# The first two weight units of a two-block transformer kernel fed by a host-turned x in eight pieces

## The chip, the cores and the metric

The kernel runs on one core of one Trainium2 chip. The metric is the device time of one execution in microseconds (us); of several runs the median is shown. The engines are TensorE (PE in the profile, PEld its weight loads), VectorE (DVE), ScalarE (ACT), GpSimd (POOL) and SyncE (SP), whose queue issues most of the loads from HBM.

## The reference, cut

One transformer block with two kinds of attention, and behind it two layers of a second kind. The change touches only the beginning of the first block: its norm over rows of x, and the product with `w_in`.

```python
def rms_norm(x, g):
    xf = x.astype(jnp.float32)
    y = xf * lax.rsqrt(jnp.mean(xf * xf, axis=-1, keepdims=True) + NORM_EPS)
    return (y * g.astype(jnp.float32)).astype(x.dtype)

u = rms_norm(h, norm_mix_g[l])                  # h = x, 256 x 1024
z = u @ w_in[l]                                 # 1024 x 5640
qa, ka, va, qk_b, vb, ob, ib, fb, ga, gb = jnp.split(z, IN_SPLITS, axis=-1)
...
i_pre = (ib + b_igate[l].astype(ib.dtype)).transpose(0, 2, 1)
f_pre = (fb + b_fgate[l].astype(fb.dtype)).transpose(0, 2, 1)
```

`ib` and `fb` are the eight gate columns of `z`. They go through a log-sigmoid and a running sum into the second attention's weights.

## The kernel before

All weights are read once, in units of 1 MB (128 partitions x 2048 float32 numbers), 227 in all. They pass through three slots: SP loads a unit into `raw`, ScalarE rounds it into `whi` (float32r), VectorE takes the rest `raw - whi` into `wlo`. TensorE forms each product from three matmuls, x_hi w_hi, x_lo w_hi and x_hi w_lo. A slot is loaded again when its `wlo` has been made (`lo_done`, in the function `fill`). A unit is 24 matmuls of 512 columns on TensorE.

Units 0 and 1 are the two halves (by rows) of `w_in`'s first 512 columns (q of the first attention), units 2 and 3 those of the next 512 (k), units 4 and 5 those of v, units 6 to 9 four narrow units of 256 columns. In the code they are called QA, KA, VA and QKB. The row factor of the norm, `rstd`, is not applied to x but later, to the products, when ScalarE copies them out of PSUM. Only the gain (`gcol`) is multiplied into x, together with its turning: TensorE transposes x (`turn_x`, four row-by-column blocks to a PSUM bank), ScalarE writes `xhi` out of PSUM and VectorE `xlo` (both in `turned_gain`).

x arrives as rows, in two halves by columns; between them come the first quarters of unit 0. TensorE first runs matmuls on zeros (`idle`), then turns the first half of x, then runs six more zero matmuls, then unit 0 in two halves (`wide_halves`), with the second half of x turned between them. Then come the eight gate matmuls (L2056: the columns of `wif` against all of x), then unit 1, then one small transpose of the convolution's weights (L2061) and two small matmuls (L2065) that add up and place the gate values. The latter wait for the table of constants (`cst_full`), which ScalarE's queue loads, 532 KB.

Each engine runs its own instructions in the order in which the code writes them; there is no scheduler. So these orders are fixed behind the head. VectorE: gate inputs (L1357, L1361), the low part of unit 4 (L1021), small steps, the rotation of q (four times L1113, L1115, L1117), the low part of unit 5, then the gates' second part that ends with four products with the identity (L1330, into `turned_a`), then the low part of unit 6. ScalarE: high part of unit 4 (L648), exp and ln of the gates (L831, L833, with a table load), the copies of q out of PSUM (L820), high part of unit 5. TensorE uses `turned_a` in L2084, which stands between units 4 and 5. GpSimd computes `rstd` from the sums of squares, makes a diagonal matrix of it (L561) and then issues some twenty small loads.

Of the kernel before, what the change touches and what calls it, by code (L numbers as in the profile page):

```python
# [11 lines left out]
ACT = mybir.ActivationFunctionType  # L12
# [3 lines left out]
P = 128  # L16
# [47 lines left out]
TURN_BANKS = {T_MIX: (4, 5, 6, 7), T_Y0: (4, 5, 2, 3), T_M0: (0, 1, 5, 7), T_M1: (0, 1, 5, 7)}  # L64
# [86 lines left out]
def turns_of(T):  # L151

    return 4 * T - (2 if T > T_Y0 else 0)
# [33 lines left out]
def build(nc, t, out):  # L187
# [7 lines left out]
    with ExitStack() as ctx:  # L195
# [113 lines left out]

        rbc0, gate_t = memT[:, 0, :], memT[0:16, 2, :]  # L310
# [39 lines left out]
        quarter_hi, quarter_full = sem("quarter_hi"), sem("quarter_full")  # L350
        half_full = [sem(f"half_full{u}") for u in range(2)]
        half_hi, half_lo = sem("half_hi"), sem("half_lo")
        x_full = [sem(f"x_full{h}") for h in range(2)]
# [46 lines left out]
        def _(sp):  # L400
# [44 lines left out]
            def half_unit(u, h, s):  # L445
                k = 4 * u + 2 * h
                sp.dma_start(raw[:, u, 1024 * h:1024 * h + 1024].rearrange("p (a b) -> p a b", a=2),
                             cols(w_in, k, 2, 0, 512)).then_inc(s, 16)

            for h in range(2):  # L450
                for r in range(RT):
                    v = slice(512 * h, 512 * h + 512)
                    sp.dma_start(res[:, r, v], t["x"][0, r * P:(r + 1) * P, v]).then_inc(x_full[h], 16)
                if h == 0:
                    for k, s in enumerate((quarter_full, half_full[0])):
                        sp.dma_start(raw[:, 0, 512 * k:512 * k + 512], w_in[P * k:P * k + P, 0:512]).then_inc(s, 16)
                    half_unit(0, 1, raw_full[0])
# [6 lines left out]
            wide(KA, w_in, 512)  # L464
# [29 lines left out]
        def _(pool):  # L494
# [64 lines left out]
            pool.wait_ge(rstd_ready, 2)  # L559
            for r in range(RT):  # L560
                pool.tensor_scalar(rdg0[:, r, :], ident, rstd[:, r:r + 1], None, ALU.mult).then_inc(diag0_ready, 1)  # L561
# [78 lines left out]
        def _(act):  # L640
# [147 lines left out]

            act.dma_start(cst[:, 0:P], t["consts"][:, 0:P]).then_inc(ident_full, 16)
            act.dma_start(gcol[:, :], t["gcol"]).then_inc(gcol_full, 16)  # L790

            act.wait_ge(pool_chain, 2)
            act.activation(cf[:, 3:4], mhalf[:, :], ACT.Square)
            def hi_half(u, h):
                v = slice(1024 * h, 1024 * h + 1024)
                if u == 0 and h == 0:

                    v = slice(512, 1024)
                act.wait_ge(raw_full[u] if h else half_full[u], 16)
                act.activation(whi[:, u, v], raw[:, u, v], ACT.Copy).then_inc(hi_done if h else half_hi, 1)  # L800
# [11 lines left out]
            turned_gain(T_MIX, N_MIX, 1)  # L812
            hi_half(1, 0)
            hi_half(1, 1)
            act.dma_start(cst[:, P:C_W], t["consts"][:, P:C_W]).then_inc(cst_full, 16)
            hi(2, 2)
# [5 lines left out]
            for u in range(PROJ):  # L822
# [3 lines left out]
                if u < PROJ - 1:  # L826
                    hi(u + 3, u % 3)
# [180 lines left out]
        def _(dve):  # L1008
# [260 lines left out]

            def lo_half(u, h):  # L1270
                v = slice(1024 * h, 1024 * h + 1024)
                dve.wait_ge(hi_done if h else half_hi, u + 1)
                dve.tensor_tensor(wlo[:, u, v], raw[:, u, v], whi[:, u, v], ALU.subtract)\
                    .then_inc(lo_done if h else half_lo, 1)

            dve.wait_ge(gcol_full, 16)
            dve.wait_ge(quarter_full, 16)
            dve.tensor_copy(whi[:, 0, 0:512], raw[:, 0, 0:512]).then_inc(quarter_hi, 1)
            turned_gain(T_MIX, N_MIX, 0, (0, 1))
# [1048 lines left out]
```

## Time and profile before

| what | value |
|---|---|
| median of 3 runs | 1345.19 us (1344.61 to 1345.22) |
| profiled execution, its own time | 1344.8 us |
| its span | 1343.0 us |
| TensorE busy | 1337.7 us, 100% of the span |
| VectorE busy | 1072.4 us, 80% |
| ScalarE busy | 702.1 us, 52% |
| HBM read | 244.45 MB, 183 GB/s over the span |

The span runs from the first instruction to the last; the own time holds 1.8 us more, which lie around it. Busy shares are means over the whole span. In this kernel they say little on the head, which is the first 60 us.

### The profile page before, as it was taken

Reading aid. Unit: us, or ns where it says so; the run is one execution under the profiler, and the core shown is the slowest. Engines: PE = TensorE matmul, PEld = TensorE weight load, DVE = VectorE, ACT = ScalarE, POOL = GpSimd, SP = SyncE. Lnnn points to the kernel's source line nnn. Section 1 sums busy time; section 2 is a strip of 40 time slices with the busy share of each in tenths; the row PEclk is TensorE's granted clock in tenths of the full one; section 3 lists DMA queues with packets and bytes.
Section 4 is the critical chain, followed back from the end, with each engine's and each line's share of the span. In section 5 each row is a group of like instructions: output and inputs, shape, how many; then the busy total and the mean of one; then the engine's idle time right before and its main releaser. Section 6 shows DMA issues by size and latency. Waiting matters only on the chain.

```text
span 1343.0 us, 17790 instructions
## 1 busy us (share of the span) xinstructions
PE 1337.7 (100%) x6477; PEld 1107.4 (82%) x6477; DVE 1072.4 (80%) x1882; ACT 702.1 (52%) x937; POOL 123.6 (9%) x158
## 2 busy tenths in 40 slices
PE   9999999999999999999999999999999999999999
PEld 7988888888888888887888888888888888888887
DVE  6994678877878877968778888898888788698777
ACT  5566446444454444577664444544445677644442
POOL 4042000020010000042000000000000332100000
PEclk9999999999999999999999999999999999999999
DMA  9654455675555555554346555465556542455562
GB/s 275 214 160 149 165 172 189 232 262 198 199 173 195 199 199 190 178 179 142 124 145 230 193 187 188 157 220 188 187 188 209 167 158 94 147 200 192 199 202 93
DMA packets 108818, 246.41 MB, mean 183 GB/s; under 512 B 5113, under 2 KB 9637, under 8 KB 108625
## 3 DMA queue, kind: packets, MB, share of 16 engines
q1 hardware_dynamic: 106576, 240.19, 53.0%
q0 software_dynamic: 1744, 4.70, 1.3%
q8 instruction: 40, 0.66, 0.2%
q10 hardware_dynamic: 432, 0.66, 0.1%
q14 instruction: 26, 0.21, 0.0%
HBM read 244.45 MB, written 1.07 MB: 183 GB/s over the span
## 4 chain that ended last, share of the span: by engine, by line
PE 97%; DVE 1%; ACT 0%; issue 0%; DMA 0%; POOL 0%; SPq 0%; DVEq 0%
PE ps L1728 27%; PE ps L1676 17%; PE ps L1678 17%; PE ps L1677 17%; PE ps L1733 14%; PE ps L1921 1%; PE ps L1702 1%; PE ps L1975 1%; PE ps L1959 1%; PE ps L2244 0%; DVE wlo L1533 0%; DMA res<-in_x 0%; PE ps L2010 0%; PE ps L2016 0%; PE ps L2020 0%
## 5 line engine op out<-in xcount | busy, mean ns | idle before, releaser
L1728 PE MATMUL ps<-whi,xx 128*128 128x512 f32 x1600 | 379.2, 389 | 0.0
L1728 PEld LDWEIGHTS ps<-whi,xx 128*128 128x128 f32 x1600 | 300.3, 188 | 62.2
L648 ACT ACTIVATE whi<-raw 128x2048 fp32r<-128x2048 f32 (+1 forms) x165 | 261.9, 1599 | 85.9 <-PE ps L1678 50.0
L1021 DVE TENSOR_TENSOR wlo<-raw,whi 128x2048 fp32r<-128x2048 f32 x105 | 240.0, 2289 | 50.6 <-ACT whi L648 49.8
L1224 DVE STREAM_TRANSPOSE sc<-sc 32x128 f32<-32x128 f32 x864 | 261.7, 303 | 12.9
L1026 DVE TENSOR_TENSOR wlo<-raw,whi 128x2048 fp32r<-128x2048 f32 x90 | 206.1, 2290 | 46.8 <-ACT whi L656 45.5
L656 ACT ACTIVATE whi<-raw 128x2048 fp32r<-128x2048 f32 x90 | 171.8, 1909 | 64.5 <-PE ps L1733 64.5
L1676 PE MATMUL ps<-whi,hhi 128*128 128x512 f32 (+1 forms) x506 | 198.3, 392 | 0.0
L1733 PE MATMUL ps<-wlo,xx 128*128 128x512 f32 x800 | 197.6, 389 | 0.0
L1678 PE MATMUL ps<-whi,hlo 128*128 128x512 f32 (+1 forms) x506 | 196.7, 389 | 0.0
L1677 PE MATMUL ps<-wlo,hhi 128*128 128x512 f32 (+1 forms) x506 | 196.5, 388 | 0.0
L1676 PE MATMUL ps<-whi,xx 128*128 128x512 f32 x464 | 187.6, 404 | 0.3 <-DVE xx L1551 0.3
L1678 PE MATMUL ps<-whi,xx 128*128 128x512 f32 x464 | 181.5, 391 | 0.0
L1677 PE MATMUL ps<-wlo,xx 128*128 128x512 f32 x464 | 180.8, 390 | 0.0
L1733 PEld LDWEIGHTS ps<-wlo,xx 128*128 128x128 f32 x800 | 150.2, 188 | 31.2
L747 ACT ACTIVATE hhi<-sc 128x512 fp32r<-128x512 f32 x54 | 34.2, 634 | 212.6 <-DVE sc L1224 212.6
L1678 PEld LDWEIGHTS ps<-whi,hlo 128*128 128x128 f32 x506 | 95.0, 188 | 19.8
L1676 PEld LDWEIGHTS ps<-whi,hhi 128*128 128x128 f32 x506 | 95.1, 188 | 19.3 <-DVE hlo L1229 0.4
L1677 PEld LDWEIGHTS ps<-wlo,hhi 128*128 128x128 f32 x506 | 95.1, 188 | 19.1
L1678 PEld LDWEIGHTS ps<-whi,xx 128*128 128x128 f32 x464 | 87.1, 188 | 19.1
L1676 PEld LDWEIGHTS ps<-whi,xx 128*128 128x128 f32 x464 | 87.3, 188 | 17.4 <-issue 1.1
L1677 PEld LDWEIGHTS ps<-wlo,xx 128*128 128x128 f32 x464 | 87.4, 188 | 16.1
(285 smaller groups left out, 1150.0 us busy)
## 6 DMA issues: line engine op xcount, KB each, us to landing
raw<-in_ffn_gate_up SPq DMA_DIRECT2D x88, 1024.0 KB, 5.2
raw<-in_ffn_w_down SPq DMA_DIRECT2D x44, 1024.0 KB, 5.0
raw<-in_w_in SPq DMA_DIRECT2D x40, 1024.0 KB, 5.1
raw<-in_gate_up SPq DMA_DIRECT2D x22, 1024.0 KB, 5.3
raw<-in_w_out SPq DMA_DIRECT2D x12, 1024.0 KB, 4.9
raw<-in_w_down SPq DMA_DIRECT2D x11, 1024.0 KB, 5.0
raw<-in_w_mem_kv SPq DMA_DIRECT2D x4, 1024.0 KB, 5.3
raw<-in_w_proj_a SPq DMA_DIRECT2D x2, 1024.0 KB, 5.2
```

What stands on the lines that cost most here:

```text
L648: ins = act.activation(whi[:, slot, v], raw[:, slot, v], ACT.Copy)
L656: act.activation(whi[:, c % 3, :], raw[:, c % 3, :], ACT.Copy).then_inc(hi_done, 1)
L747: act.activation(hhi[:, par, :], hidT, ACT.Copy).then_inc(h_hi, 1)
L1021: dve.tensor_tensor(wlo[:, u % 3, v], raw[:, u % 3, v], whi[:, u % 3, v], ALU.subtract)\
L1026: dve.tensor_tensor(wlo[:, c % 3, :], raw[:, c % 3, :], whi[:, c % 3, :], ALU.subtract)\
L1224: ins = dve.transpose(dst[32 * a:32 * a + 32, :, b, :], src[32 * b:32 * b + 32, :, a, :])
L1676: pe.matmul(o, stat[0], mov[0], start=start, stop=False)
L1677: pe.matmul(o, stat[0], mov[1], start=False, stop=False)
L1678: return pe.matmul(o, stat[1], mov[0], start=False, stop=stop)
L1702: ins = pe.transpose(ps[:, bank, a:a + P], res[:, r, P * c:P * c + P], ident)
L1728: pe.matmul(ps[:, banks[r], :], x(4 * half + k, P * r, P)[part], whi[:, slot, 512 * k:512 * k + 512], start=half == 0 and k == 0 and part ...
L1733: ins = pe.matmul(ps[:, banks[r], :], x(4 * half + k, P * r, P)[0], wlo[:, slot, 512 * k:512 * k + 512], start=False, stop=half == 1 and k ...
```

## The change

- The host gives x a second time, turned: `x_t`, 128 x 8 x 256. It is loaded in eight pieces of 128 KB into the tile `memT` (called `xt` there), and each is followed in SP's queue by a piece of 256 KB of unit 0 or 1.
- ScalarE makes `xhi` of a piece from `xt` by a copy with the gain as scale, and VectorE `xlo`; TensorE's 16 transposes, and the last six zero matmuls with one of the first eight, are gone.
- TensorE multiplies piece by piece: high, low weights of the piece before, low x.
- x in rows, which the sums of squares and the residual still need, is loaded behind unit 2. Unit 2 and unit 3 are now loaded and split in halves, and unit 3 stands behind x.
- The gate matmuls come behind unit 1 and not behind unit 0; the two small matmuls (L2065) come behind unit 2 and not ahead of it. VectorE's gate inputs stand ahead of unit 4's low part as before.
- In ScalarE's queue `gcol` is issued ahead of the identity. The constants are issued behind the wait for x in rows.

```diff
+            for c in range(KC):
+                x_part(c)
+                w_part(c // 4, c % 4)
             sp.dma_start(wif[:, :, :], t["wif"]).then_inc(wif_full, 16)
-            half_unit(1, 0, half_full[1])
-            half_unit(1, 1, raw_full[1])
+            half_unit(KA, 0)
+            half_unit(KA, 1)
+            for r in range(RT):
+                sp.dma_start(res[:, r, :], t["x"][0, r * P:(r + 1) * P, :]).then_inc(x_full, 16)
...
+            half_unit(KA + 1, 0)
+            half_unit(KA + 1, 1)
             wide(VA, w_in, 1024)
...
             act.wait_ge(gcol_full, 16)
-            turned_gain(T_MIX, N_MIX, 0, (0, 1))
-            hi_half(0, 0)
-            turned_gain(T_MIX, N_MIX, 0, (2, 3))
-            hi_half(0, 1)
+            for c in range(KC):
+                act.wait_ge(xt_full[c], 16)
+                act.activation(xhi[:, c, :], xt[:, c, :], ACT.Copy, scale=gain_col(N_MIX, c)).then_inc(xhi_done, 1)
+                if c < KC - 1:
+                    hi_part((c + 1) // 4, (c + 1) % 4)
             act.wait_ge(wif_full, 16)
             act.activation(wifs[:, :, 0:8], wif[:, :, :], ACT.Copy).then_inc(wif_hi, 1)
-            act.wait_ge(x_full[0], 16 * RT)
-            act.wait_ge(x_full[1], 16 * RT)
+            hi_half(KA, 0)
+            hi_half(KA, 1)
+            act.wait_ge(x_full, 16 * RT)
...
+            for c in range(KC):
+                dve.wait_ge(xhi_done, c + 1)
+                dve.scalar_tensor_tensor(out=xlo[:, c, :], in0=xt[:, c, :],
+                                         scalar=gain_col(N_MIX, c), in1=xhi[:, c, :], op0=ALU.mult, op1=ALU.subtract)\
+                    .then_inc(xlo_done, 1)
+                lo_part(c // 4, c % 4)
...
+                if u == 0:
+                    gate_sums()
+                    lo_half(KA + 1, 0)
+                    lo_half(KA + 1, 1)
+                if u == 1:
+                    gate_inputs()
+                if 0 < u < 7 and u != 4:
                     lo(u + 3)
...
-            idle(8)
...
+            idle(7)
...
-            pe.wait_ge(ident_full, 16)
-            turn_x(0)
-            idle(6)
+            for c in range(KC):
+                high(c)
+                if c > 0:
+                    w_low(c - 1)
+                x_low(c)
+            w_low(KC - 1)
```

TensorE's first instructions, before the change (`pr` is the tile of zeros, `res` is x in rows, `xx` holds `xhi` and `xlo`):

```order
L1983 MATMUL ps<-pr 128x128 [waits warm_ready]
L1983 MATMUL ps<-pr 128x128 x7
L1994 MATMUL ps<-cst,res 128x128 [waits x_full0,ident_full]
L1994 MATMUL ps<-cst,res 128x128 x7
L1983 MATMUL ps<-pr 128x128 x6
L2010 MATMUL ps<-whi,xx 128x512 [waits xhi_done,quarter_hi]
```

And of the change:

```order
L2019 MATMUL ps<-pr 128x128 [waits warm_ready]
L2019 MATMUL ps<-pr 128x128 x6
L2035 MATMUL ps<-whi,xx 128x512 [waits xhi_done,quarter_hi]
L2035 MATMUL ps<-whi,xx 128x512
L2041 MATMUL ps<-whi,xx 128x512 [waits xlo_done]
L2041 MATMUL ps<-whi,xx 128x512
L2035 MATMUL ps<-whi,xx 128x512 [waits xhi_done,part_hi]
```

The transposes and the second run of zeros are gone; after the second pair TensorE waits for a second piece.

TensorE around the end of unit 1, before the change (L1676 is the first matmul of unit 2):

```order
L2020 MATMUL ps<-wlo,xx 128x512 x3
L2061 MATMUL ps<-cst,cwr 128x32 [waits bias_full]
L2065 MATMUL ps<-cst,memT 128x8 [waits gate_copied,cst_full]
L2065 MATMUL ps<-cst,memT 128x8
L1676 MATMUL ps<-whi,xx 128x512 [waits lo_done]
```

Of the change, from the end of unit 2 to unit 3's first matmul:

```order
L1714 MATMUL ps<-whi,xx 128x512
L2105 MATMUL ps<-cst,memT 128x8 [waits gate_copied,cst_full]
L2105 MATMUL ps<-cst,memT 128x8
L2111 MATMUL ps<-memT,cst 128x128 [waits diag0_ready]
L2111 MATMUL ps<-memT,cst 128x128
L1712 MATMUL ps<-whi,xx 128x512 [waits half_lo]
```

The two small gate matmuls (L2065, now L2105) stand one whole unit later.

VectorE around the gates, before the change (`small` holds the gates):

```order
L1294 COPY memT<-ps 16x256 [waits gate_ps]
L1296 TENSOR_TENSOR memT<-memT,ps 16x256 [waits gate_copied]
L1021 TENSOR_TENSOR wlo<-raw,whi 128x2048 [waits hi_done] x2
L1357 SCALAR_TENSOR_TENSOR small<-ps,rstd,bif 128x8 [waits gate_ps,bias_full,rstd_ready]
L1357 SCALAR_TENSOR_TENSOR small<-ps,rstd,bif 128x8
```

Of the change, from the sums of squares to unit 4's low part:

```order
L1318 ISA xn,ss<-res 128x1024 [waits x_full]
L1318 ISA ss 128x1
L1323 COPY memT<-ps 16x256 [waits gate_ps]
L1325 TENSOR_TENSOR memT<-memT,ps 16x256 [waits gate_copied]
L1301 TENSOR_TENSOR wlo<-raw,whi 128x1024 [waits half_hi]
L1301 TENSOR_TENSOR wlo<-raw,whi 128x1024 [waits hi_done]
L1332 SCALAR_TENSOR_TENSOR small<-ps,rstd,bif 128x8 [waits gate_ps,bias_full,rstd_ready]
L1332 SCALAR_TENSOR_TENSOR small<-ps,rstd,bif 128x8
L1336 SCALAR_TENSOR_TENSOR small<-small 128x8 [waits gate_dve]
L1338 TENSOR_SCALAR small<-small 128x8
L1038 TENSOR_TENSOR wlo<-raw,whi 128x2048 [waits hi_done,dve_chain]
```

The gate inputs keep their place ahead of unit 4's low part, but what they wait for on TensorE has moved; the gates' sums now stand ahead of unit 3's low part.

## Rows read from the trace of the kernel before

**Rows 1.** The page: the span, TensorE's busy time, and its clock by slices.

```profile
span 1343.0 us, 17790 instructions
...
PE 1337.7 (100%) x6477; PEld 1107.4 (82%) x6477; DVE 1072.4 (80%) x1882; ACT 702.1 (52%) x937; POOL 123.6 (9%) x158
...
PEclk9999999999999999999999999999999999999999
```

**Rows 2.** TensorE's waits, the second longest: us in total, times, longest.

```profile
PE ps L1921 <- DVE sc L1188: 0.5, 1, 0.5
```

**Rows 3.** Timeline, first 11 us: start, us, engine, line, operation, tiles.

```profile
1.06 3.79 PE L1983 MATMUL ps<-pr 128*128 128x128 f32 x16 [1.06 <-DVE pr L1268]
...
5.08 1.41 PE L1994 MATMUL ps<-cst,res 128*128 128x128 f32 x8 [0.24 <-DMA res<-in_x]
...
5.67 0.43 DVE L1278 CAST whi<-raw 128x512 fp32r<-128x512 f32 x1 [4.67 <-DMA raw<-in_w_in]
...
6.33 1.50 PE L1983 MATMUL ps<-pr 128*128 128x128 f32 x12
...
6.90 0.62 ACT L800 ACTIVATE whi<-raw 128x512 fp32r<-128x512 f32 x1
...
7.59 1.17 PE L2010 MATMUL ps<-whi,xx 128*128 128x512 f32 x4
...
10.44 1.03 PE L1994 MATMUL ps<-cst,res 128*128 128x128 f32 x8
```

**Rows 4.** Timeline, 14 to 28 us, TensorE.

```profile
14.05 2.01 PE L2056 MATMUL ps<-xx,wifs 128*16 128x512 f32 x8
...
21.53 0.59 PE L2065 MATMUL ps<-cst,memT 16*128 16x8 f32 x4
...
22.04 0.50 PE L1676 MATMUL ps<-whi,xx 128*128 128x512 f32 x1
...
27.62 0.60 PE L2071 MATMUL ps<-memT,cst 128*128 128x128 f32 x4
```

**Rows 5.** Timeline, 24 to 29 us, VectorE and ScalarE.

```profile
24.14 1.92 ACT L648 ACTIVATE whi<-raw 128x2048 fp32r<-128x2048 f32 x1 [2.21 <-DMA raw<-in_w_in]
...
24.18 0.35 DVE L1357 SCALAR_TENSOR_TENSOR small<-ps,rstd,bif 128x8 f32<-128x8 f32 x2
...
24.57 0.17 DVE L1361 SCALAR_TENSOR_TENSOR small<-small 128x8 f32<-128x8 f32 x1
...
25.97 0.19 ACT L831 ACTIVATE small<-small 128x8 f32<-128x8 f32 x1
...
28.87 0.69 DVE L1113 TENSOR_TENSOR sq<-work,cst 128x512 f32<-128x512 f32 x1 [0.23 <-ACT work L820]
```

**Rows 6.** Timeline, 36 to 40 us.

```profile
36.12 2.50 DVE L1330 TENSOR_TENSOR turned_a<-cst,small 128x512 fp32r<-128x512 f32 x4
...
39.23 2.29 DVE L1021 TENSOR_TENSOR wlo<-raw,whi 128x2048 fp32r<-128x2048 f32 x1 [0.61 <-ACT whi L648]
...
39.46 1.10 PE L2084 MATMUL ps<-turned_a,hhi 128*128 128x512 f32 x4
```

**Rows 7.** Timeline, 49 to 54 us.

```profile
49.87 2.29 DVE L1021 TENSOR_TENSOR wlo<-raw,whi 128x2048 fp32r<-128x2048 f32 x1
...
53.29 0.36 PE L1676 MATMUL ps<-xx,whi 128*128 128x256 f32 x1
```

**Rows 8.** DMA issues of two short windows: count, KB each, median us to landing.

```profile
raw<-in_w_in SPq DMA_DIRECT2D x1, 256.0 KB, 3.9
...
cst<-in_consts ACTq DMA_DIRECT2D x1, 532.0 KB, 6.6
```

**Rows 9.** Stretches: engines' busy time, granted clock, DMA share, GB/s.

```profile
0.00:5.00 5.00, 3.79 (x16) 3.49 (x16) 0.17 (x1) 1.49 (x2) 0.32 (x6) 1.00 0.64 188
...
8.00:16.00 8.00, 8.00 (x41) 5.91 (x40) 7.38 (x13) 6.29 (x12) 3.63 (x6) 1.00 1.05 383
...
26.00:34.00 8.00, 8.00 (x41) 6.75 (x40) 7.47 (x10) 4.88 (x8) 0.58 (x2) 1.00 1.01 162
```

More of the change, by code:

```diff
@@ L151, in turns_of @@
 def turns_of(T):
-    return 4 * T - (2 if T > T_Y0 else 0)
+    return 4 * T - (6 if T > T_Y0 else 4)
 def s_bank(i):
@@ L794, in hi_half @@
             def hi_half(u, h):
+                act.wait_ge(raw_full[u % 3] if h else half_full[u - KA], 16 * (u // 3 + 1) if h else 16)
+                if u == 3 and h == 0:
+                    act.wait_ge(unit_used, 1)
                 v = slice(1024 * h, 1024 * h + 1024)
[L796 to L800, printed above, removed]
+                act.activation(whi[:, u % 3, v], raw[:, u % 3, v], ACT.Copy).then_inc(hi_done if h else half_hi, 1)
@@ L825, in _ @@
                     evac_pT(8)
-                if u < PROJ - 1:
+                if u == 0:
+                    hi_half(KA + 1, 0)
+                    hi_half(KA + 1, 1)
+                elif u < PROJ - 1:
                     hi(u + 3, u % 3)
@@ L1268, in _, with lo_part @@
             dve.memset(pr[:, 0, 0:P], 0.0).then_inc(warm_ready, 1)
+            def lo_part(u, k):
+                if u == 0 and k == 0:
+                    dve.wait_ge(quarter_hi, 1)
+                elif k == 3:
+                    dve.wait_ge(hi_done, u + 1)
+                else:
+                    dve.wait_ge(part_hi, k + 1 + 2 if u else k)
+                v = slice(512 * k, 512 * k + 512)
+                dve.tensor_tensor(wlo[:, u, v], raw[:, u, v], whi[:, u, v], ALU.subtract)\
+                    .then_inc(lo_done if k == 3 else part_lo, 1)
@@ new lines, in gate_inputs @@
+            def gate_inputs():
+                dve.wait_ge(rstd_ready, 2)
+                dve.wait_ge(bias_full, 48)
+                dve.wait_ge(gate_ps, 3)
+                for r in range(RT):
+                    ins = dve.scalar_tensor_tensor(out=gates[:, r, :], in0=ps[:, 4, 8 * r:8 * r + 8],
+                                                   scalar=rstd[:, r:r + 1], in1=bif[:, :], op0=ALU.mult, op1=ALU.add)
+                ins.then_inc(gate_dve, 1)
+                dve.wait_ge(gate_dve, 1)
+                dve.scalar_tensor_tensor(out=rh(0), in0=f_pre, scalar=-1.0, in1=f_pre, op0=ALU.mult, op1=ALU.max)\
+                    .then_inc(gate_dve, 1)
+                link(dve.tensor_scalar(rh(72), f_pre, 0.0, None, ALU.min))
@@ L1985, in _ @@
             pe.wait_ge(warm_ready, 1)
-            idle(8)
-            def turn_x(half):
-                pe.wait_ge(x_full[half], 16 * RT)
-                for b in (2 * half, 2 * half + 1):
-                    for c in (2 * half + b, 2 * half + b + 2):
-                        bank, a = turn_at(T_MIX, c)
-                        for r in range(RT):
-                            ins = pe.transpose(ps[:, bank, a + P * r:a + P * r + P], res[:, r, P * c:P * c + P], ident)
-                    ins.then_inc(tr_ps, 1)
@@ L2026, in _, with high @@
-            pe.wait_ge(ident_full, 16)
-            turn_x(0)
-            idle(6)
+            idle(7)
+            def high(c):
+                u, k = c // 4, c % 4
+                if c == 0:
+                    pe.wait_ge(quarter_hi, 1)
+                elif k == 3:
+                    pe.wait_ge(hi_done, u + 1)
+                else:
+                    pe.wait_ge(part_hi, k + 3 if u else k)
+                pe.wait_ge(xhi_done, c + 1)
+                for r in range(RT):
+                    pe.matmul(ps[:, r, :], x(c, P * r, P)[0], w(u, 512 * k, 512)[0], start=c == 0, stop=False)
@@ new lines, in x_low, with w_low @@
+            def x_low(c):
+                pe.wait_ge(xlo_done, c + 1)
+                for r in range(RT):
+                    pe.matmul(ps[:, r, :], x(c, P * r, P)[1], w(c // 4, 512 * (c % 4), 512)[0], start=False, stop=False)
+            def w_low(c):
+                u, k = c // 4, c % 4
+                pe.wait_ge(lo_done if k == 3 else part_lo, u + 1 if k == 3 else 3 * u + k + 1)
+                for r in range(RT):
+                    ins = pe.matmul(ps[:, r, :], x(c, P * r, P)[0], w(u, 512 * k, 512)[1], start=False, stop=c == KC - 1)
+                if k == 3:
+                    ins.then_inc(unit_used, 1)
@@ L2308 @@
     given["wif"] = np.asarray(inputs["w_in"])[0][:, 3584:3592].reshape(KC, P, 2 * BH).transpose(1, 0, 2)
+    given["x_t"] = np.asarray(inputs["x"])[0].reshape(SEQ, KC, P).transpose(2, 1, 0)
     given["mem_t"] = np.asarray(inputs["mem_2"])[0].reshape(SEQ, KC, P).transpose(2, 1, 0)
```

132 lines of the change are left out of this document (49 added, 83 removed).

## The prediction

> **What bounds the kernel now.** The page first [rows 1]: TensorE is busy for 1337.7 of 1343.0 us, with the clock granted in full in every slice. Then its waits [rows 2]: behind the start the longest is 0.5 us in all. So anything TensorE does earlier, and keeps, comes off the end; nothing else does. What can be kept is decided in the head, so I went to the timeline.
>
> TensorE runs zero matmuls from 1.06 us, turns x from 5.08, runs zeros again from 6.33 and starts unit 0 at 7.59 [rows 3]. From there it never stops: the second turning at 10.44 [rows 3], gates at 14.05, unit 2 at 22.04, and that unit's 24 matmuls end at 27.62, so 5.58 us a unit and 0.2325 us a matmul [rows 4]. What could be gained is what stands ahead of 22.04 and is not a weight matmul.
>
> Then I looked for the place where another engine is nearly late. It is between units 4 and 5. TensorE's product with `turned_a` starts at 39.46. VectorE has finished writing that tile at 36.12 + 2.50 = 38.62 [rows 6]. That is 0.84 us of slack. The next is unit 7, whose low part ends at 49.87 + 2.29 = 52.16 for a matmul at 53.29 [rows 7], 1.13 us. VectorE is occupied nearly without a break between 28.9 and 52, so this work comes earlier only if its first link does. That link is the rotation at 28.87, which waits for q's copy by ScalarE. The copy stands behind ln and exp of the gates, exp at 25.97, which stands behind the high part of unit 4 (24.14 to 26.06) and behind the gate inputs (24.18, the last that matters ends at 24.57 + 0.17 = 24.74) [rows 5]. Those need TensorE's two small gate matmuls, done at 21.53 + 0.59 = 22.12 [rows 4].
>
> **The change, part by part.**
>
> *Start.* The first `w` piece is now SP's second load, with 0.13 MB ahead of it; before it was the third, issued at 1.65 us, with 0.52 MB ahead, and was there for the cast at 5.67 [rows 3, 8]. It is issued 0.45 us earlier, and about 0.4 MB less lies ahead, which at 0.35 MB per us is 1.1 us. If only the issue counts it lands at 5.2, if both count in full at 4.1; I take the smaller amount of data alone, 4.5, since in these first us the bytes are what fills the time. The cast costs 0.43 [rows 3]: first matmul at 5.0 instead of 7.59 (4.6 to 5.7). The x piece and `gcol`, now first in its queue, are there by then.
>
> *The first two pieces.* The sixteen rows of zeros from 1.06 took 3.79 us, the twelve from 6.33 took 1.50 [rows 3]: 0.237 against 0.125 each, the levels of 1.2 and 2.4 GHz. The rise came between 5.1 and 6.3, after 4 us of nearly unbroken work. So the first four matmuls run at about 0.46 us and end at 6.8. The second weight piece lands about 1.1 us behind the first, at 5.6; ScalarE then needs 0.62 for it [rows 3] and about 0.43 for its x: 6.7. TensorE goes on at 6.8, and at the upper level from here.
>
> *Steady pieces.* A piece is 0.393 MB, 1.06 us at 0.37 MB per us (a little under the 383 GB/s of 8 to 16 us [rows 9], as a third of it comes in rows of 1 KB). ScalarE and VectorE need about 1.05 us each. TensorE needs 6 x 0.2325 = 1.40 us. It sets the pace: 44 matmuls are 10.2 us, to 17.0. Eight gate matmuls, 1.86, and the small transpose, 0.1: unit 2 starts at 19.0 and not at 22.04. Unit 2 ends at 24.6, the small gate matmuls, now here, at 25.1, and unit 3 starts at about 25.4. The 16 transposes and the zeros are thus worth 2.6 us at this place.
>
> *Loads.* 0.94 MB are in by 5 us (188 GB/s x 5 [rows 9]); the eight pieces and `gcol`, 3.25 MB, by 11.2; unit 2 by 13.9; x in rows by 16.7; unit 3 by 19.4. One more MB is loaded than before, but units 2 and 3 come ahead of their use by 5 us, which covers their split in halves (about 1 us on ScalarE and 1.2 us on VectorE a half). The constants are issued when x is in, at 16.7. They took 6.6 us before [rows 8], issued then as now into a queue with two units in front: 23.3, and with unit 4 (1.6 MB, 4.2 us) all is in by 23.6. They are wanted at 24.6. I cost this at nothing. If they come later, every us counts, as all of the gates' chain stands behind it. GpSimd's diagonal and its twenty small loads move back by about 5 us; nobody waits for them before unit 3.
>
> *The chain.* The gate inputs now start when TensorE is done with the small matmuls, at 25.1, and not at 24.18. Exp can follow 0.6 us later, at 25.7, instead of 25.97. The other condition, unit 4's high part, ends at 23.6 + 1.9 = 25.5. So the rotation starts about 0.27 us earlier, not 2.6, and `turned_a` is ready at about 38.35. TensorE would want it at 39.46 - 2.6 = 36.9. It waits some 1.5 us there. The gain that passes is 0.84 + 0.27 less about 0.1 for the handover: **1.0 us**. At unit 7 VectorE has lost its 0.61 us of idle [rows 6], so its work is 0.9 us ahead and the slack of 1.13 holds. From there on VectorE follows TensorE, and the gain stays to the end.
>
> The sum: 1344.8 of the profiled execution less 1.0 is 1343.8. The median of the runs was 1345.19, 0.4 above it, so I say **1344.2**.
>
> *A rule against pieces.* The rows show loads of 256 KB landing 3.9 us after their issue [rows 8] while others are issued meanwhile. The Trainium skill, "DMA: Bandwidth & Descriptors", Anatomy of one DMA, gives each DMA about 2 us that do not depend on its size, and puts the half-efficient size at some 860 KB; these pieces are far below. By that rule alone, sixteen loads one behind the other would take about 39 us (an estimate from the page), and the head would lose some 25 us instead of gaining. The stretch of 383 GB/s is against it.
>
> **The rivals.**
>
> *The whole head gain passes.* If the slack at `turned_a` or the order on VectorE is not what I read, the end moves by 2.6: 1342.6. For it: TensorE waits for nothing now. Against: the 0.84 us are plain arithmetic on two rows. Chance 0.10.
>
> *The clock rises late.* TensorE now has a gap from about 4.3 to 5.0 and perhaps one at 6.5, where it had 0.24 us idle before [rows 3]. Each us that the rise comes after 6.8 costs half a us, with nothing to hide it, since the chain hangs on TensorE. If it comes as late as 11.5, the loss is 2.35: 1.0 - 2.35, so 1346.6, slower than before. It decides from 2 us behind 6.8 on. The Trainium skill, "TensorE: Matmul & The Clock Gate", What's actually happening, says that the gate follows how busy the array has lately been; by that rule the gaps matter, and the rise may shift from run to run. In the trace a gap did not stop it. Chance 0.13.
>
> *The constants are late.* If GpSimd's small loads, which ran beside a stretch of only 162 GB/s at 26 to 34 us [rows 9], slow this stretch instead, the 1.6 MB of unit 4 and constants from 19.4 need 9.9 us: 29.3 and not 23.6. The small matmuls come 4.7 us late, and the result is 3.7 slower: 1348.9. It is slower than before as soon as they land after 25.6. A mild form, 0.5 to 1.5 us late, gives 1344.7 to 1345.7. Chance 0.11, a third of it the full form.
>
> *The pieces come one by one.* Each load waits for the one before: sixteen times 3.9 us, 62 us instead of 11: some 50 us slower, 1395. Chance 0.01.
>
> **How the numbers follow.** My forecast has 0.63; its own range is 1343.6 (first piece at 4.1 and unit 4 loaded 0.4 earlier) to 1344.9 (first piece at 5.2). The remaining 0.02 is unnamed. The range reaches down to the full gain and up to the late clock: 1342.4 to 1346.6, which leaves out less than 2 in 10. Two tenths of a per cent, 2.7 us, is about what a measurement of this kernel tells from no change. Faster by that needs under 1342.5, the lower half of the first rival and a little: 0.06. Slower needs over 1347.9: the full form of the constants, a still later clock, the serial pieces, 0.07. Within: 0.87.
>
> **What would show it.** Right: the first 512-column matmul at 5.0; a pause of up to 0.3 us behind the fourth; unit 2 at 19.0, unit 3 at 25.4; the small gate matmuls not waiting for a load; the list of waits with a new line, TensorE for VectorE's `turned_a`, of about 1.5 us; that product at 38.4. Wrong: no such wait and `turned_a` written before 37; a wait on the constants; zeros' successors at 0.46 us beyond 8 us; or TensorE waiting for pieces 2 to 7. The time would be wrong without a change in mechanism if the waits of later blocks, small now, should grow.

## The result, and the profile after

The changed kernel takes 1346.76 us (median of 20 runs, 1345.66 to 1348.41), the kernel before 1344.64 (20 runs, 1344.22 to 1345.95). The ratio is 1.0016, with a 95% interval of 1.001 to 1.0022: 2.1 us slower, and 0.16 us above the range. The prediction had added 0.4 us to its sum because the three runs that it had of the kernel before had their median at 1345.19; over 20 runs that median is 1344.64, so against its own base the range ended 1.4 us above the kernel before, and the changed kernel is 2.1 above it. The profiled execution took 1347.21 us, 2.4 more than the 1344.8 of the one before.

The page of the changed kernel, the lines that answer to [rows 1]:

```profile
span 1345.4 us, 17755 instructions
...
PE 1337.4 (99%) x6447; PEld 1105.7 (82%) x6447; DVE 1072.7 (80%) x1888; ACT 703.6 (52%) x942; POOL 124.2 (9%) x158
...
PEclk9999999999999999999999999999999999999999
```

TensorE's busy time is down by only 0.3 us, though 16 transposes and 14 rows of zeros are gone. (It counts matmuls at the lower clock with their full length.) Its waits (us in total, times, longest) show what is new:

```profile
PE ps L2124 <- DVE turned_a L1372: 1.4, 1, 1.4
PE ps L2035 <- DVE whi L1306: 1.1, 1, 1.1
...
PE ps L2035 <- ACT xx L821: 0.4, 1, 0.4
```

The first is the wait that was forecast. The other two are in the first 8 us. The changed kernel's timeline there, and to 20 us (start, us, engine, line, operation):

```profile
1.06 3.36 PE L2019 MATMUL ps<-pr 128*128 128x128 f32 x14 [1.06 <-DVE pr L1285]
...
5.05 0.43 DVE L1306 CAST whi<-raw 128x512 fp32r<-128x512 f32 x1 [4.05 <-DMA raw<-in_w_in]
...
5.53 1.22 PE L2035 MATMUL ps<-whi,xx 128*128 128x512 f32 x2 [1.12 <-DVE whi L1306]
...
6.55 1.05 PE L2041 MATMUL ps<-whi,xx 128*128 128x512 f32 x2
6.87 0.63 ACT L809 ACTIVATE whi<-raw 128x512 fp32r<-128x512 f32 x1 [2.09 <-DMA raw<-in_w_in]
...
8.04 1.19 PE L2035 MATMUL ps<-whi,xx 128*128 128x512 f32 x2 [0.43 <-ACT xx L821]
...
9.03 1.05 PE L2048 MATMUL ps<-wlo,xx 128*128 128x512 f32 x2
...
9.88 1.05 PE L2041 MATMUL ps<-whi,xx 128*128 128x512 f32 x2
...
10.74 1.05 PE L2035 MATMUL ps<-whi,xx 128*128 128x512 f32 x2
...
12.26 0.63 PE L2041 MATMUL ps<-whi,xx 128*128 128x512 f32 x2
...
12.73 0.63 PE L2035 MATMUL ps<-whi,xx 128*128 128x512 f32 x2
...
20.02 2.01 PE L2095 MATMUL ps<-xx,wifs 128*16 128x512 f32 x8
```

Pairs that start 0.86 us apart (9.03, 9.88, 10.74) are at 1.2 GHz, pairs 0.47 apart (12.26, 12.73) at 2.4. So the level rose at about 12.0 us. The clock row of the page and of the windows reads full here from the start; only the spacing of the rows shows the level. From 12.26 on, 34 matmuls take 7.76 us, 0.228 each, without a wait.

The changed kernel, 19 to 43 us. The rows answer to [rows 4 to 6]:

```profile
19.12 1.06 ACT L829 ACTIVATE xn<-res 128x1024 f32<-128x1024 f32 x1 [1.50 <-DMA res<-in_x]
...
22.14 0.50 PE L1712 MATMUL ps<-whi,xx 128*128 128x512 f32 x1
...
26.99 1.91 ACT L660 ACTIVATE whi<-raw 128x2048 fp32r<-128x2048 f32 x1 [3.08 <-DMA raw<-in_w_in]
...
27.81 0.61 PE L2105 MATMUL ps<-cst,memT 16*128 16x8 f32 x4
...
28.56 0.36 DVE L1332 SCALAR_TENSOR_TENSOR small<-ps,rstd,bif 128x8 f32<-128x8 f32 x2 [3.36 <-PE ps L2105]
...
29.15 0.21 ACT L848 ACTIVATE small<-small 128x8 f32<-128x8 f32 x1 [0.24 <-DVE small L1336]
...
32.07 0.69 DVE L1130 TENSOR_TENSOR sq<-work,cst 128x512 f32<-128x512 f32 x1 [0.31 <-ACT work L834]
...
39.33 2.50 DVE L1372 TENSOR_TENSOR turned_a<-cst,small 128x512 fp32r<-128x512 f32 x4
...
41.88 1.21 PE L2124 MATMUL ps<-turned_a,hhi 128*128 128x512 f32 x4 [1.41 <-DVE turned_a L1372]
```

Unit 2 starts at 22.14; before it was 22.04 [rows 4]. All that was removed is lost again by then, and the 0.5 us of the small gate matmuls too, which no longer stand ahead of unit 2. The rotation moved from 28.87 [rows 5] to 32.07, and TensorE's product with `turned_a` from 39.46 [rows 6] to 41.88, 2.42 later. That shift stays to the end: the spans differ by 2.4.

The loads of the changed kernel (count, KB each, us to landing): the first two pieces of weights, issued at 1.17 and 2.11 us, then the constants, issued at 19.16. Behind them the stretches (engines' busy time, granted clock, DMA share, GB/s):

```profile
raw<-in_w_in SPq DMA_DIRECT2D x1, 256.0 KB, 3.8
...
raw<-in_w_in SPq DMA_DIRECT2D x1, 256.0 KB, 4.7
...
cst<-in_consts ACTq DMA_DIRECT2D x1, 532.0 KB, 7.6
```

```profile
0.00:5.00 5.00, 3.36 (x14) 3.06 (x14) 0.17 (x1) 1.99 (x3) 0.32 (x6) 1.00 0.62 164
5.00:8.00 3.00, 2.07 (x4) 1.16 (x4) 1.50 (x4) 1.09 (x3) 0.00 (x0) 1.00 1.00 354
8.00:12.00 4.00, 3.96 (x9) 3.14 (x10) 4.00 (x8) 3.96 (x8) 0.00 (x0) 1.00 1.06 379
...
20.00:24.00 4.00, 4.00 (x18) 2.36 (x17) 2.31 (x6) 2.40 (x4) 3.13 (x6) 1.00 1.06 404
24.00:28.00 4.00, 4.00 (x20) 3.06 (x18) 1.20 (x2) 1.01 (x1) 4.00 (x8) 1.00 1.02 351
```

The constants, issued at 19.2 when x had landed, took 7.6 us and were there at 26.8. Before they took 6.6 [rows 8]. The DMA engines were busy in full all that time, at 351 to 404 GB/s, so the number of bytes ahead is the likely cause of the lateness; two experiments below take bytes away.

### The profile page after: what moved, and what is told of

It reads as the page before. It is cut to its first block, busy times and chain, and to the rows that moved or that the text cites. A ratio compares the mean times of both kernels' runs of the same rounds, so it can differ in the third digit from the quotient of the medians.

```text
span 1345.4 us, 17755 instructions
## 1 busy us (share of the span) xinstructions
PE 1337.4 (99%) x6447; PEld 1105.7 (82%) x6447; DVE 1072.7 (80%) x1888; ACT 703.6 (52%) x942; POOL 124.2 (9%) x158
## 4 chain that ended last, share of the span: by engine, by line
PE 96%; DVE 2%; ACT 1%; issue 1%; DMA 0%; POOL 0%; SPq 0%; DVEq 0%
PE ps L1764 27%; PE ps L1712 17%; PE ps L1714 17%; PE ps L1713 17%; PE ps L1769 13%; PE ps L1957 1%; PE ps L1738 1%; PE ps L2011 1%; PE ps L1995 1%; PE ps L2284 0%; DVE wlo L1569 0%; DMA raw<-in_w_in 0%; PE ps L2035 0%; PE ps L2048 0%; PE ps L2041 0%
## 5 line engine op out<-in xcount | busy, mean ns | idle before, releaser
L660 ACT ACTIVATE whi<-raw 128x2048 fp32r<-128x2048 f32 (+1 forms) x163 | 258.1, 1595 | 83.0 <-PE ps L1714 50.3
L1038 DVE TENSOR_TENSOR wlo<-raw,whi 128x2048 fp32r<-128x2048 f32 x103 | 235.3, 2288 | 46.5 <-ACT whi L660 45.7
L1043 DVE TENSOR_TENSOR wlo<-raw,whi 128x2048 fp32r<-128x2048 f32 x90 | 206.0, 2289 | 46.8 <-ACT whi L668 45.7
```

The costliest lines, as they stand in the source:

```text
L660: ins = act.activation(whi[:, slot, v], raw[:, slot, v], ACT.Copy)
L1038: dve.tensor_tensor(wlo[:, u % 3, v], raw[:, u % 3, v], whi[:, u % 3, v], ALU.subtract)\
L1043: dve.tensor_tensor(wlo[:, c % 3, :], raw[:, c % 3, :], whi[:, c % 3, :], ALU.subtract)\
```

## The experiments

There are twelve kernels, in three groups (four experiments, four, four). Each was timed 11 times, and each group beside 33 runs of the kernel before, whose medians were 1344.82, 1344.87 and 1344.85 us. A time is the median, with lowest and highest, and a ratio stands to the kernel before, with its 95% interval. Two questions came first. Is it the late clock? And what does the move of the small gate matmuls cost by itself?

### Zeros in both gaps of the head

```diff
-            idle(7)
+            idle(10)
...
                 x_low(c)
+                if c == 0:
+                    for _ in range(5):
+                        pe.matmul(ps[:, 7, 0:P], pr[:, 0, 0:P], pr[:, 0, 0:P], start=True, stop=True)
```

> The changed kernel with ten pairs of zero matmuls at the start instead of seven, and five pairs on a free PSUM bank between the first and the second x piece, so that TensorE has hardly a gap before 8 us. Theory 'clock': the late rise to the upper level (12.0 us in the changed kernel) is what the head lost. Then the 512-column matmuls step at 0.23 us from about 6 us on, unit 1 ends near 18.2, unit 2 starts near 20.2, and the small gate matmuls wait for the constants (landed at 26.8): gate inputs at 26.6 to 27.5 instead of 28.56, time 1.0 to 2.0 us under the changed kernel: 1344.8 to 1345.8. Rival 'loads': the pieces come too late anyway; then the time stays within 0.5 us of the changed kernel (1346.8) whatever the clock does.

Measured: 1347.65 us (1345.56 to 1348.25), ratio 1.0014 [1.0005, 1.0023]. The head did what was expected: the first pair of unit 0 starts at 5.04 and the next at 5.61, so the level is up. But the median is not the 1344.8 to 1345.8 of the theory; it is 0.9 over the changed kernel. This kernel's timeline, 25 to 42 us:

```profile
25.80 0.61 PE L2108 MATMUL ps<-cst,memT 16*128 16x8 f32 x4
...
26.70 1.92 ACT L660 ACTIVATE whi<-raw 128x2048 fp32r<-128x2048 f32 x1 [3.14 <-DMA raw<-in_w_in]
...
28.52 0.19 ACT L848 ACTIVATE small<-small 128x8 f32<-128x8 f32 x1
...
41.22 1.88 PE L2127 MATMUL ps<-turned_a,hhi 128*128 128x512 f32 x4 [2.78 <-DVE turned_a L1372]
```

TensorE's gate matmuls are 2.0 us earlier than in the changed kernel. But exp (28.52) now stands behind the high part of unit 4, whose load is not there before 26.70. So exp is only 0.6 us earlier, and the wait for `turned_a` grows from 1.4 to 2.8 us. What follows that wait, in stretches of this kernel:

```profile
38.00:41.50 3.50, 0.72 (x3) 0.30 (x3) 3.40 (x9) 0.00 (x0) 0.00 (x0) 1.00 0.85 88
41.50:44.90 3.40, 3.40 (x9) 2.63 (x9) 3.37 (x4) 1.91 (x1) 0.00 (x0) 0.50 0.98 300
44.90:48.00 3.10, 3.10 (x15) 2.52 (x15) 3.00 (x6) 0.00 (x0) 0.00 (x0) 1.00 1.00 342
```

The granted clock is 0.50, the level of 1.2 GHz, for 3.4 us: 1.7 us lost. The times fall in two groups. Five runs with a mean granted clock of 1.000 lie at 1345.56 to 1346.19; six with 0.998 or 0.999 at 1347.65 to 1348.25. Half the clock for 3.4 us of 1346 is a mean of 0.9987, so here the mean tells one group from the other. In the five runs without a fall the median is 1345.87, 0.5 under the changed kernel's runs at a mean of 1.000 (1346.38). That is all that the filled gaps gained.

### Zeros in the first gap alone

The same, with only `idle(7)` made `idle(10)`.

> The changed kernel with ten pairs of zero matmuls at the start instead of seven; the pause behind the first piece (7.4 to 8.0 us in the changed kernel) stays. Theory 'clock, first gap': the gap of 1.1 us ahead of the first matmul alone kept the clock down: rise near 6, time as with both gaps filled, 1344.8 to 1345.8. Rival 'clock, both gaps': the pause behind the first piece, now 1.6 us long, brings it down again or keeps it down; rise near 12 again and time near 1346.8.

Measured: 1347.39 us (1345.51 to 1348.97), ratio 1.0016 [1.0007, 1.0025]. The level rose at about 4.2 us, as with both gaps filled, and stayed up through a wait of 1.6 us at 6.5. So the second gap alone doesn't bring the level down again. That the first alone caused the late rise is not shown by one profile of each (more in the part on why the prediction was wrong). The wait for `turned_a` was 1.9 us, and the clock fell again behind it, from 41.7 to 45.1. Of its runs, the five at 1.000 lie up to 1346.57 (median 1346.26, only 0.1 under the changed kernel's) and the six at 0.999 from 1347.39 on.

### The kernel before with a gap in its zeros

```diff
-            idle(8)
+            idle(5)
...
             turn_x(0)
-            idle(6)
```

> The kernel before with five pairs of zeros at the start instead of eight and none behind the first turning, so with a gap of about 1.8 us ahead of the first transpose and nothing else changed. Theory 'clock': the rise moves from 5.8 us to 9 or later, the matmuls of unit 0 step at 0.43 us, and since TensorE never waits the whole delay comes out at the end: 1.0 to 2.5 us over the kernel before (1344.6): 1345.6 to 1347.1. Rival: the level comes back by itself near 6 us and the time is that of the kernel before, or up to 0.5 less as the first matmul starts earlier.

Measured: 1345.32 us (1344.51 to 1345.94), ratio 1.0003 [0.9994, 1.0013]. The level rose at about 7.8, behind a gap of 1.2 us, and not at 9 or later, and the time is 0.5 over the kernel before and not 1.0 to 2.5: the theory missed. The five profiles that begin like the kernel before and have no such gap (its own and four of the experiments below) have the rise between 5.8 and 7.2 us, so this one is late by 0.6 to 2.

### The kernel before with the small gate matmuls behind unit 2

```diff
                     pe.transpose(ps[:, 5, 0:32], cwr[:, :], ident[0:32, 0:32]).then_inc(gate_ps, 1)
+                if u == 2:
                     pe.wait_ge(cst_full, 16)
                     pe.wait_ge(gate_copied, 2)
```

> The kernel before with one part of the change alone: the two small gate matmuls (with their wait for the constants) stand behind unit 2 and not ahead of it. Theory 'chain': the gate inputs start at 27.7 instead of 24.18, the rotation at 31.2 instead of 28.87, turned_a is ready at 40.95 instead of 38.62, TensorE waits 1.5 us for it between units 4 and 5, and the time is 1.5 us over the kernel before: 1346.1. Rival 'slack': VectorE catches up, no wait, time unchanged within 0.3 us.

Measured: 1346.76 us (1346.19 to 1347.35), ratio 1.0014 [1.0005, 1.0023]. This kernel's timeline, 27 to 42 us:

```profile
27.49 0.61 PE L2066 MATMUL ps<-cst,memT 16*128 16x8 f32 x4
...
28.23 0.36 DVE L1357 SCALAR_TENSOR_TENSOR small<-ps,rstd,bif 128x8 f32<-128x8 f32 x2 [3.81 <-PE ps L2066]
...
31.74 0.69 DVE L1113 TENSOR_TENSOR sq<-work,cst 128x512 f32<-128x512 f32 x1 [0.37 <-ACT work L820]
...
41.55 1.19 PE L2085 MATMUL ps<-turned_a,hhi 128*128 128x512 f32 x4 [1.42 <-DVE turned_a L1330]
```

With the head, the loads and the transposes of the kernel before, this one move costs 1.9 us (1.5 was expected), nearly as much as the whole change loses. TensorE here has no earlier start to set against it, and in the changed kernel's profile it had none either. The chain is the one of the prediction: gate inputs 28.23, rotation 3.51 us behind (3.51 in the changed kernel too), product 9.8 us behind that.

### Covering the wait with zeros

Eight zero matmuls ahead of the `turned_a` product: first with the zeros of the first experiment, then in the changed kernel as it is (five there). The second of the two thus has the changed kernel's head, loads and order, and shows a second execution of them.

```diff
                 if u == 4:
+                    for _ in range(8):
+                        pe.matmul(ps[:, 7, 0:P], pr[:, 0, 0:P], pr[:, 0, 0:P], start=True, stop=True)
                     pe.wait_ge(gate_dve, 5)
```

> e1_zeros_both with eight pairs of zero matmuls more, on a free PSUM bank directly ahead of the product with turned_a, so that TensorE's wait of 2.8 us there holds work. Theory 'second fall': that wait brought the clock down for 3.4 us (41.5 to 44.9 in e1's profile), worth 1.5 to 1.7 us, in about half of e1's runs (their times stand in two groups, 1345.6 to 1346.2 and 1347.7 to 1348.3). Then no fall, one group, median 1345.6 to 1346.2. Rival: the two groups come from when the loads land; then they remain and the median stays near 1347.6.

> The changed kernel with five pairs of zero matmuls directly ahead of the product with turned_a and nothing else. The profiled execution of the changed kernel had no fall of the clock there, so what remains is the late first rise: theory 'chain plus now and then a fall': the runs above 1347.5 vanish, the median moves from 1346.8 to 1346.2 to 1346.7. Rival: unchanged spread, 1345.7 to 1348.4.

Measured: 1346.24 us (1345.47 to 1347.75), 1.0012 [1.0003, 1.0021], for the first. All its 11 runs have a mean clock of 1.000, so the fall is gone. But 1346.24 is no better than the first experiment's undisturbed runs (median 1345.87), and one run of the 11 took 1347.75 without any fall. For the second: 1346.46 (1345.78 to 1348.34), 1.0014 [1.0005, 1.0023], 0.3 under the changed kernel with intervals that overlap. One run lies above 1348, so the slow runs did not vanish. Four of its 11 runs read 0.999; where the clock was low in these isn't shown. (In its profile the five zero matmuls left 0.8 us of the wait.) A late first rise is not it: the changed kernel's profile has its rise at 12.0 and reads 1.000.

The profile of the second, 1345.99, is worth more than its median. Its rows:

```profile
5.07 1.22 PE L2035 MATMUL ps<-whi,xx 128*128 128x512 f32 x2 [0.66 <-DVE whi L1306]
...
8.46 0.86 PE L2048 MATMUL ps<-wlo,xx 128*128 128x512 f32 x2
9.16 0.63 PE L2041 MATMUL ps<-whi,xx 128*128 128x512 f32 x2
...
20.38 0.50 PE L1712 MATMUL ps<-whi,xx 128*128 128x512 f32 x1
...
26.06 0.52 PEld L2105 LDWEIGHTS ps<-cst,memT 16*128 16x128 f32 x4 [0.35 <-DMA cst<-in_consts]
...
26.07 1.91 ACT L660 ACTIVATE whi<-raw 128x2048 fp32r<-128x2048 f32 x1 [3.58 <-DMA raw<-in_w_in]
...
27.89 0.19 ACT L848 ACTIVATE small<-small 128x8 f32<-128x8 f32 x1
...
30.79 0.69 DVE L1130 TENSOR_TENSOR sq<-work,cst 128x512 f32<-128x512 f32 x1 [0.23 <-ACT work L834]
```

With the same head the level rose at about 9.0 and not at 12.0, and unit 2 starts at 20.38 and not 22.14. Now the small gate matmuls do wait for the constants, and exp stands behind the high part of unit 4, whose load is not there before 26.07. The rotation is 1.28 us earlier than in the changed kernel's profile, and the time 1.22 less. It is still 1.1 over the kernel before, and that part is set by loads.

### Half a MB less ahead of unit 4

On top of the first of these two, the second half of x's rows is loaded behind unit 5. The kernel leaves out their sum of squares and takes that of the first half twice:

```diff
-            for r in range(RT):
-                sp.dma_start(res[:, r, :], t["x"][0, r * P:(r + 1) * P, :]).then_inc(x_full, 16)
+            sp.dma_start(res[:, 0, :], t["x"][0, 0:P, :]).then_inc(x_full, 16)
...
             wide(VA, w_in, 1024)
+            sp.dma_start(res[:, 1, :], t["x"][0, P:2 * P, :]).then_inc(x_late, 16)
```

> f1_zeros_wait with the second 128 rows of x loaded behind unit 5 instead of ahead of unit 3, 0.5 MB less in front of unit 4 and of the constants. The second rows' sum of squares is taken from the first rows, so the row factors of the second half are others. Theory 'loads': unit 4's load (26.6 in e1) sets exp and so turned_a; it lands 1.3 earlier, the gate inputs start near 25.5 to 26.5, exp at 27.1, and the time falls by 1.0 to 1.4 under f1: 1344.4 to 1345.0. Rival 'TensorE': the gate matmuls set it; time within 0.3 of f1.

Measured: 1345.37 us (1344.94 to 1346.28), 1.0004 [0.9995, 1.0013]. That is 0.87 less than its base, where 1.0 to 1.4 was expected; ten of its 11 runs lie under the base's median. Unit 4's high part starts at 25.70 and not 26.37, and the rotation at 30.60 and not 31.09. The bytes are a cost, a little smaller than I had said. With them gone, the gate matmuls (26.34) and unit 4 (25.70) are again about even.

### The kernel before, with its zeros removed behind the turning

`idle(8)` becomes `idle(9)` and `idle(6)` goes. Does an early start alone gain?

> The kernel before without the six pairs of zeros behind the first turning, and one pair more at the start against the gap. Unit 0 can start near 6.7 instead of 7.59. Theory 'slack at turned_a': up to 0.84 us of that pass to the end: 0.4 to 0.8 us under the kernel before. Rival 'clock': with less work ahead the level rises later and the time is the same or up to 0.5 over it.

Measured: 1344.95 us (1344.3 to 1346.38), 1.0002 [0.9993, 1.0011]: missed. This kernel's timeline, 5 to 11 us:

```profile
6.84 0.70 PE L2010 MATMUL ps<-whi,xx 128*128 128x512 f32 x2
7.98 0.70 PE L2010 MATMUL ps<-whi,xx 128*128 128x512 f32 x2 [0.44 <-ACT whi L800]
...
10.35 1.03 PE L1994 MATMUL ps<-cst,res 128*128 128x128 f32 x8
```

Unit 0 starts 0.75 us earlier than before, but waits for its second piece of weights. The second turning stands at 10.35 against 10.44 [rows 3]. The twelve rows of zeros in the kernel before had lain in time in which TensorE would have waited for the next load. Their removal brings the second turning 0.1 us forward and not the 1.5 that they take, and the median shows no gain.

### VectorE's second gate part ahead of unit 5's low part

```diff
-                if u == 3:
+                if u == 2:
                     dve.wait_ge(cst_full, 16)
                     dve.wait_ge(gate_ps, 4)
```

It was tried in three kernels: on the previous experiment, on the first one, and on the kernel before alone.

> f4_before_early with VectorE's second gate part (small steps and turned_a) ahead of unit 5's low part instead of behind it. Theory 'slack at turned_a': f4's head start of 0.75 us was swallowed there (its profile waits 0.6 us for turned_a). With the order turned, turned_a is ready 2.3 us earlier and the tightest places are unit 5 and unit 7 with 1.7 us, so the start passes: 0.5 to 0.8 us under the kernel before (1344.87): 1344.1 to 1344.4. Rival: something else holds f4, time as f4, 1344.95.

> e1_zeros_both with the same turned order on VectorE. Theory 'chain from unit 4's load': the rotation starts at 31.2 as in e1, turned_a is ready at 38.9 where TensorE wants it at 38.7, and unit 5's low part at 41.2, 0.8 later than the kernel before has unit 5 on TensorE: 0.6 to 1.1 us over the kernel before, 1345.5 to 1346.0, one group of times, no wait over 1.6 us. Rival: the second fall of the clock comes all the same; median 1347 or more.

> The kernel before with the turned order on VectorE alone. No engine waits less ahead of TensorE, which is never idle: time within 0.3 us of the kernel before. If it is slower, unit 5's low part, now 3.4 us later (38.6 for a start at 40.4), is late in some runs.

| on | us | ratio |
|---|---|---|
| before without `idle(6)` | 1344.79 (1344.57 to 1345.43) | 0.9999 [0.999, 1.0008] |
| changed, zeros in both gaps | 1345.43 (1345.02 to 1346.6) | 1.0004 [0.9995, 1.0013] |
| before | 1345.15 (1344.79 to 1345.51) | 1.0001 [0.9992, 1.001] |

In the first, `turned_a` is no longer waited for, but as said there was nothing to pass on (product at 39.20 against 39.46). In the second the median is 0.4 under the first experiment's undisturbed runs, and its 11 runs all have a mean clock of 1.000. In its profile, 1346.6 and its highest run, unit 4 came only at 27.64; the waits were 1.7 for `turned_a` and 1.0 for unit 5's low part. Here too unit 4's load sets exp (29.46). In the third the 0.3 us over the kernel before are within the noise.

### The constants split

On top of the second row of the table: two masks of the table, 0.26 MB, are loaded behind unit 5's high part (the waits for `cst_full` go to 32 with it).

```diff
-            act.dma_start(cst[:, P:C_W], t["consts"][:, P:C_W]).then_inc(cst_full, 16)
+            for a, b in ((C_TRI, C_MB), (C_INV, C_W)):
+                act.dma_start(cst[:, a:b], t["consts"][:, a:b]).then_inc(cst_full, 16)
...
+                if u == 2:
+                    for a, b in ((C_MA, C_TRI), (C_MB, C_INV)):
+                        act.dma_start(cst[:, a:b], t["consts"][:, a:b]).then_inc(cst_rest, 16)
```

> g2_zeros_swap with the two masks of the table of constants (0.26 of 0.53 MB) loaded behind unit 5's high part. Theory 'loads': 0.26 MB less ahead of unit 4 and the constants, unit 4 lands 0.7 earlier, exp and the rotation 0.4 to 0.7 earlier, the time 0.3 to 0.7 under g2: 1345.0 to 1345.4. Rival 'TensorE': no change against g2.

Measured: 1344.73 us (1344.13 to 1347.23), 1.0 [0.9991, 1.0009], 0.7 under its base, the upper end of what was expected; eight of its 11 runs lie under the base's fastest. Its timeline, 25 to 39 us:

```profile
25.86 1.91 ACT L661 ACTIVATE whi<-raw 128x2048 fp32r<-128x2048 f32 x1 [2.61 <-DMA raw<-in_w_in]
...
35.62 2.49 DVE L1377 TENSOR_TENSOR turned_a<-cst,small 128x512 fp32r<-128x512 f32 x4
...
38.63 1.10 PE L2133 MATMUL ps<-turned_a,hhi 128*128 128x512 f32 x4
```

`turned_a` is ready at 38.1, half a us ahead of its use; what TensorE still waits for is unit 5's low part, 0.6 us. The 2.0 us to the changed kernel are recovered, by three edits: zeros in the head, the order on VectorE, and fewer bytes ahead of unit 4. That is level with the kernel before, not ahead of it.

## Why the prediction was wrong

**What held.** TensorE waits for nothing else behind the head, and the place that decides is the product with `turned_a`. The chain from the small gate matmuls over exp and the rotation to `turned_a` was read rightly, and the forecast wait of 1.5 us measured 1.4. That the two agree is in part luck, for both ends of the wait came about as late, TensorE by 3.6 us (40.5 for 36.9) and `turned_a` by 3.5. The one-part kernel shows that the move of those matmuls behind unit 2 alone costs 1.9 us. The prediction put it into its sum, but against a TensorE that would be there early. The pieces did not come one by one either: in the stretch of pieces the DMA engines moved 379 GB/s. The Trainium skill's rule in "DMA: Bandwidth & Descriptors", Anatomy of one DMA, speaks against loads this small. The page gives it for loads that GpSimd issues; for these, which SP queues one behind the other, this trace does not bear it out.

**The step that failed first: "The first two pieces".** It said: "TensorE goes on at 6.8, and at the upper level from here." It went on at 8.04 (1.24 us later), and the ten matmuls from there to 12.26 took 4.22 us and not 2.33 (1.89 more). Together that is 3.13, and unit 2 came 3.14 late, at 22.14 and not 19.0. The start of it was a load. The prediction let the first weight piece gain from the 0.4 MB less ahead of it and put it at 4.5. It took 3.8 us from its issue, and 3.9 before [rows 8]: only the earlier issue counted, so the cast began at 5.05 (the prediction had 5.2 for this case). The second piece took 4.7 us, was taken up at 6.87 and not 5.6, and so TensorE stood still for 1.1 us where I had reckoned with 0.7, and for 0.4 us ahead of the second piece, where the prediction had at most 0.3.

The late rise goes with such gaps, but its size is not fixed. By the spacing of the rows in all 14 profiles of this case, the level rose between 4.0 and 7.2 us in the eleven in which TensorE had no gap over 0.3 us ahead of it (six of these begin with the same ten pairs of zero matmuls, and they alone cover 4.0 to 7.2). In the three with a longer gap it rose at 7.8 (gap of 1.2), 9.0 (0.7) and 12.0 (1.1). The last two have the same head. So a rise at 6.8 was within what a head without gaps does, and this head has gaps. The rival "the clock rises late" named this place and 1346.6 as its time. It had the smaller chance because "a gap did not stop it" in the trace before; that gap was 0.24 us.

**The step that failed beside it: "Loads".** It had the constants and unit 4 in by 23.6. They were there at 26.8 and 27.0. 2.4 us of that is x's rows landing at 19.1 and not at 16.7, mostly since the pieces took 13.1 us and not 11.2 (the last weight piece is taken up at 13.13). Here too the sum counted only the bytes ahead. By 12 us the DMA engines had moved 3.4 MB (164, 354 and 379 GB/s over 5, 3 and 4 us), more than the 3.25 of the pieces; loads issued behind the pieces were moving beside them. A further 1.0 is the constants' own flight, 7.6 for 6.6. In the profiled execution of the changed kernel this lateness is masked: exp starts at 29.15 because of TensorE, but unit 4's high part ends at 28.90, so a TensorE that came earlier could bring exp forward by only 0.25 us with this load. That is why zeros in the head gained so little: 1345.87 in undisturbed runs against 1346.38. In six of the eight profiles with the changed kernel's loads or nearly these (all but its own and that with half a MB less) exp stands directly behind unit 4's high part, and in the same six the small gate matmuls wait for the constants. The x loaded twice is part of it: half a MB less was worth 0.87, 0.26 MB less 0.7.

This is nearly what the rival "the constants are late" named as slower (landing after 25.6; chance 0.11, and for a mild form 1344.7 to 1345.7). Its mechanism, GpSimd's small loads slowing the stretch, is not what the profile shows: from 20 to 24 us and from 24 to 28 us, where GpSimd issues them (from 22.99 on), the DMA engines moved 404 and 351 GB/s and not 162.

**Adding up.** Gate inputs at 28.56 and not 25.1, 3.46 late; `turned_a` at 41.83 and not 38.35, 3.48 late; the profiled execution at 1347.21 and not 1343.8, 3.41 late. All of the error lies ahead of the gate inputs. It went from a gain of 1.0 to a loss of 2.4. The profile with the same head and an earlier rise divides it: its exp stands at 27.89, held by the load, and its time is 1345.99. So of the 3.4 us about 2.2 belong to the late loads and 1.2 to the later rise of the clock on top of them. That rests on one profile of each. In 7 of the 20 runs of the changed kernel the mean granted clock was 0.997 to 0.999, with a median of 1348.05; in the other 13 it was 1.000, with 1346.38. So spells at the lower clock may make up 0.4 us of the median. But three of the seven (1346.68 to 1346.77) lie among the 13, which reach 1347.53, so other differences, the time of the rise among them, are as large. Where the spells lie isn't shown: the profiled run had none behind the head, and covering the wait left four such runs in 11.

**The zeros behind the turning.** The prediction names them beside the transposes as what is "worth 2.6 us". Its 19.0 for unit 2 is built from landings and matmuls and holds no term for them, so this is not where it failed. But the name misleads: in the kernel before they covered a wait for weights, and their 1.5 us could not have been gained (10.35 against 10.44).

**Open.** Why the level rose at 7.8 in the kernel with a gap of 1.2 us, at 12.0 in the changed one with gaps of 1.1 and 0.4, and at 9.0 with the same head and gaps of 0.7 and 0.3; each is one profile. Not tried: the changed head with the small gate matmuls left ahead of unit 2, for which the constants would have to be issued earlier than x's rows.

## What to carry to other kernels

Filler work on an engine costs only what it exceeds the wait that it covers; before its time is counted as a gain, ask when the next operand lands. When a small step is moved by one unit, take its whole chain to the next place with little slack: here 0.84 us of slack on one tile was all that a forecast head start of 2.6 us could have used. And where two conditions of one step lie within half a us of one another (TensorE's gates, unit 4's load), mending one gains at most that half us; sum up the bytes ahead of the second before the first is touched, and count those issued close behind too. Where a time hangs on the clock's rise, give it a range, not a point: here heads of the same code differed by 3 us.

## What the runs showed of the hardware

- One wait of TensorE in full run can bring its clock down. Behind a wait of 2.8 us it was granted 0.50 for 3.4 us, behind one of 1.9 us (the second experiment) as long; behind 1.4 us (the changed kernel's profile) and 1.7 us (zeros with the swap) it stayed at 1.00. It is not so in every execution: in the first two experiments five runs of 11 each have a mean of 1.000. The Trainium skill, "TensorE: Matmul & The Clock Gate", HAM oscillation, describes it for a loop that waits for each load; these traces show it for one wait of a kernel whose TensorE is 99% busy.
- The head's rise came between 4.0 and 7.2 us without a gap over 0.3 us (11 profiles), and at 7.8, 9.0 and 12.0 with a gap of 0.7 to 1.2 us (3 profiles). Section What's actually happening of that page of the Trainium skill lets the clock follow recent activity and vary from run to run, and the traces agree with both. In the changed kernel's profile the late rise cost ten matmuls nearly twice their time (4.22 us for 2.33).
- In the first 5 us fewer bytes ahead did not bring a load in sooner: the first 256 KB of weights landed 3.8 us behind their issue with 0.13 MB ahead of them in SP's queue, and 3.9 us with 0.52 MB ahead.
- A run's mean granted clock, to three digits, tells of a fall of 3.4 us: in the first two experiments it divides the 22 runs without an overlap in time. It does not tell of a late first rise (1.000 with the rise at 12.0), and in the changed kernel the two groups overlap.
